# Two decoder layers on one core: down rows in 16 KB pieces, third norm's first half moved beside the last output product, slots computed before gates

## The reference, cut to what matters

```python
x = x + swa(rms_norm(x, od_norm1))        # 16 query heads, 2 key/value heads of 64, window 128
h = rms_norm(x, od_norm2)                 # the third norm that the kernel turns by transposes
logits = h @ w_router                     # 8 experts
top_val, top_idx = lax.top_k(logits, 2)
gates = softmax(top_val) placed at top_idx
for e in range(8):
    y = y + gates[..., e:e+1] * ((silu(h @ w1[e]) * (h @ w3[e])) @ w2[e])   # w1, w3: 1024 x 3584, w2: 3584 x 1024
x = x + y
```

## Time and profile before

| | |
|---|---|
| three runs | 1455.85, 1457.12, 1460.83 us; median 1457.12 |
| profiled execution | 1462.09 us, span 1460.3 us, granted TensorE clock 0.995 |
| busy in the span | PE 1441.4 (99%), PEld 1200.4, DVE 1133.1 (78%), ACT 944.8 (65%), POOL 35.4 |
| DMA | 437.21 MB, 299 GB/s over the span; q1, SP's queue: 180496 packets, 426.11 MB |
| split of half a unit, mean | VectorE 2.272 us (406 of them), ScalarE 1.898 us |
| attention layer / routing / experts | from about 402 / 486 / 508 us on |

### The profile page before, as it was taken

One profiled execution on the slowest core, in us unless ns is written; L12 is line 12 of the kernel. 1 busy time (PEld: TensorE's weight loads), 2 busy tenths in 40 slices (PEclk: granted clock), 3 DMA queues, 4 the chain that ended last, 5 costly groups with the idle time before them and its releaser, 6 DMA issues.

```text
span 1460.3 us, 19714 instructions
## 1 busy us (share of the span) xinstructions
PE 1441.4 (99%) x7542; PEld 1200.4 (82%) x7542; DVE 1133.1 (78%) x968; ACT 944.8 (65%) x844; POOL 35.4 (2%) x22
## 2 busy tenths in 40 slices
PE   9999999999999999999999999999999999999998
PEld 7998888888886787887888888888888888888886
DVE  6985664454476788988888898888888888898895
ACT  7633643443476766766777777777777777677774
POOL 0000000000000000000000001000000000000000
PEclk9999999999999999999999999999999999999999
DMA  9510666544542499999999999999999999999993
GB/s 360 206 58 28 237 220 219 191 172 146 176 162 83 152 362 364 386 364 348 377 368 386 391 373 380 372 375 376 386 383 372 387 393 367 386 389 372 369 391 149
DMA packets 183873, 437.21 MB, mean 299 GB/s; under 512 B 4880, under 2 KB 6416, under 8 KB 183824
## 3 DMA queue, kind: packets, MB, share of 16 engines
q1 hardware_dynamic: 180496, 426.11, 79.1%
q0 software_dynamic: 2336, 8.39, 2.1%
q10 hardware_dynamic: 992, 2.05, 0.4%
HBM read 431.29 MB, written 5.24 MB: 299 GB/s over the span
## 4 chain that ended last, share of the span: by engine, by line
PE 83%; issue 8%; DMA 4%; DVE 4%; ACT 1%; POOL 0%; DVEq 0%; ACTq 0%; SPq 0%; POOLq 0%
PE ps L272 26%; PE ps L274 25%; PE ps L273 25%; DMA raw<-in_od_moe_w 3%; DVE wlo L261 1%; PE ps L452 1%; DMA out<-arena,slot_tok 1%; ACT whi L255 1%; PE ps L991 1%; PE ps L840 0%; PE ps L1188 0%; DVE hTlo L316 0%; PE ps L2102 0%; DVE small L1418 0%; PE ps L333 0%
## 5 line engine op out<-in xcount | busy, mean ns | idle before, releaser
L261 DVE TENSOR_TENSOR wlo<-raw,whi 128x2048 fp32r<-128x2048 f32 x406 | 905.8, 2272 | 170.6 <-ACT whi L255 168.3
L255 ACT CAST whi<-raw 128x2048 fp32r<-128x2048 f32 x406 | 750.5, 1898 | 210.8 <-DMA raw<-in_od_moe_w 151.3
L272 PE MATMUL ps<-whi,hThi 128*128 128x512 f32 (+1 forms) x1240 | 490.2, 395 | 0.3
L274 PE MATMUL ps<-whi,hTlo 128*128 128x512 f32 (+1 forms) x1240 | 482.7, 389 | 0.0
L273 PE MATMUL ps<-wlo,hThi 128*128 128x512 f32 (+1 forms) x1240 | 482.5, 389 | 0.0
L274 PEld LDWEIGHTS ps<-whi,hTlo 128*128 128x128 f32 x1240 | 233.6, 188 | 48.7
L272 PEld LDWEIGHTS ps<-whi,hThi 128*128 128x128 f32 x1240 | 233.8, 189 | 47.3 <-issue 1.2
L273 PEld LDWEIGHTS ps<-wlo,hThi 128*128 128x128 f32 x1240 | 233.9, 189 | 45.8 <-issue 0.2
L272 PE MATMUL ps<-whi,aThi 128*128 128x512 f32 x560 | 219.3, 392 | 0.0
L274 PE MATMUL ps<-whi,aTlo 128*128 128x512 f32 x560 | 218.2, 390 | 0.0
L273 PE MATMUL ps<-wlo,aThi 128*128 128x512 f32 x560 | 217.9, 389 | 0.0
(11 more groups left out here) (308 smaller groups left out, 759.4 us busy)
## 6 DMA issues: line engine op xcount, KB each, us to landing
raw<-in_od_moe_w SPq DMA_DIRECT2D x168, 2048.0 KB, 9.6
raw<-in_ev_ffn_w SPq DMA_DIRECT2D x21, 2048.0 KB, 7.8
raw<-in_ev_w_in SPq DMA_DIRECT2D x6, 2048.0 KB, 13.1
raw<-in_ev_w_out SPq DMA_DIRECT2D x2, 2048.0 KB, 8.5
raw<-in_od_w_in SPq DMA_DIRECT2D x2, 2048.0 KB, 7.8
raw<-in_od_w_out SPq DMA_DIRECT2D x2, 2048.0 KB, 8.1
raw<-in_ev_w_in SPq DMA_DIRECT2D x2, 1024.0 KB, 8.6
xres<-in_x SPq DMA_DIRECT2D x2, 512.0 KB, 4.3
```

The lines of the kernel that those rows point to most:

```text
L255: act.copy(whi[s][:, part], raw[s][:, part]).then_inc(hi_ready, 1)
L261: dve.tensor_tensor(wlo[s][:, part], raw[s][:, part], whi[s][:, part].bitcast(F32), ALU.subtract).then_inc(lo_ready, 1)
L272: pe.matmul(to, lhi, rhi, start=first, stop=False)
L274: return pe.matmul(to, llo, rhi, start=False, stop=last)
```

## The change

It has five parts. (a) `w2m` gives partition p the rows 4p to 4p+3 of a block of 512 instead of rows p, 128+p, 256+p, 384+p, so that a partition's 16 KB lie together in DRAM; the gate product writes its column 4i+c to place c*128+i, so that the transposed blocks fit these rows. (b) ScalarE's and VectorE's parts of the first half of norm 3 stand ahead of the squares and of the last addition, VectorE's split of U_MOE is cut in two around them, and on TensorE the second half is turned behind the router's and `dense`'s first two k instead of ahead of them. (c) The second tile of scaled rows is made behind the copy of the router rows; `dense` of tile 1 gives five k instead of four ahead of the rank products. (d) The gates are computed behind the slots and expert 0's `select` (`gate_values`), with a semaphore `tok_ready` for TensorE's `index`. (e) The second half of norm 2 is turned behind `keys_values`' first two k instead of ahead of them.

```diff
+        def by_row(t):
+            return t.rearrange("p (i c) -> p i c", c=FC)
+        def by_block(t):
+            return t.rearrange("p (c i) -> p i c", c=FC)
-        def dve_scaled(dve, by):
-            for t in range(TT):
+        def dve_scaled(dve, by, tiles):
+            for t in tiles:
...
-        w2m = a["od_moe_w2"][0].rearrange("e (b c p) n -> (e b) p c n", p=P, c=FC)
+        w2m = a["od_moe_w2"][0].rearrange("e (b p c) n -> (e b) p c n", p=P, c=FC)
...
-                    dve.tensor_tensor(actf[0:CAP, t, :], sil[0:CAP, t, :], H3[t][0:CAP, :], ALU.mult).then_inc(a_ready, 1)
+                    dve.tensor_tensor(by_block(actf[0:CAP, t, :]), by_row(sil[0:CAP, t, :]), by_row(H3[t][0:CAP, :]),
+                                      ALU.mult).then_inc(a_ready, 1)
...
             hi_u(act, U_MOE)
+            act_turned(act, 3, 0)
             for t in range(TT):
                 act_square(act, 3, 0, t)
             act_square(act, 3, 1, 0)
-            act.wait_ge(unit_used, U_ROUTER)
-            act_turned(act, 3, 0)
...
                 if n == 3:
-                    lo_u(dve, U_MOE)
+                    split_lo(dve, U_MOE, U_MOE % NS, halves=(0,))
+                    dve_turned(dve, 3, 0)
...
-            dve_turned(dve, 3, 0)
+            split_lo(dve, U_MOE, U_MOE % NS, halves=(1,))
         def odd_tensor(pe):
-            pe_turn_x(pe, 2, 1)
...
                         if b == 3:
                             ins.then_inc((qkv_ps, unit_used)[t], 1)
+                    if b == 0:
+                        pe_turn_x(pe, 2, 1)
...
-            dve_scaled(dve, route_gain)
+            dve_scaled(dve, route_gain, (0,))
...
             dve.tensor_copy(by_expert, ps[4][0:NE, 0:T]).then_inc(rt_rows, 1)
+            dve_scaled(dve, route_gain, (1,))
...
-            dve.wait_ge(rt_exp, 1)
...
             dve.wait_ge(rank_ps, 1)
...
+            def gate_values():
+                dve.wait_ge(rt_exp, 1)
...
+                dve.tensor_tensor(tok_gate[:, :, 0:NE, 1], gate, tmp, ALU.add).then_inc(tok_ready, 1)
...
                 select(q, 0, n0)
                 if q == 0:
+                    gate_values()
                     split_lo(dve, U_MOE + 1, 1)
...
         def experts_tensor(pe):
-            pe_turn_x(pe, 3, 1)
...
-            early, late = range(KD // 2), range(KD // 2, KD)
+            early, late = range(KD // 2 + 1), range(KD // 2 + 1, KD)
...
-            pe.wait_ge(hT_ready, 12 + 2)
             for b in range(4):
                 pe.wait_ge(hT_ready, 12 + b + 1)
...
                 if b < 3:
                     dense(0, (2 * b, 2 * b + 1))
+                if b == 0:
+                    pe_turn_x(pe, 3, 1)
...
                 pe.wait_ge(sel_ready, 2 * n + 2)
+                pe.wait_ge(tok_ready, 1)
```

More of the change, by code:

```diff
@@ L1686, in build_program @@
         rt_rows, rt_ps, first_sil, sil_ps = sem("rt_rows rt_ps first_sil sil_ps")
-        old_in, y_half = sem("old_in y_half")
+        old_in, y_half, tok_ready = sem("old_in y_half tok_ready")
         sil_slots = actf[0:CAP, 1, :]
@@ L1944, in experts_vector @@
             link(dve.tensor_tensor(slot_of[:, :, 0:NE], tmp, ahead, ALU.add))
+            def gate_values():
+                dve.wait_ge(rt_exp, 1)
+                link(dve.tensor_scalar(v[0], second, 1.0, None, ALU.add))
+                link(dve.reciprocal(v[0], v[0]))
+                link(dve.tensor_tensor(v[1], second, v[0], ALU.mult))
+                link(dve.tensor_tensor(gate, oh1, along(v[0], NE), ALU.mult))
+                link(dve.tensor_tensor(tmp, oh2, along(v[1], NE), ALU.mult))
+                dve.tensor_tensor(tok_gate[:, :, 0:NE, 1], gate, tmp, ALU.add).then_inc(tok_ready, 1)
             def select(q, e, n):
@@ L2010, in moe @@
                     dve.wait_ge(sil_ready, tiles(0, 0, 0))
-                    dve.tensor_tensor(actf[0:CAP, 0, :], sil_slots, H3[0][0:CAP, :], ALU.mult).then_inc(a_ready, 1)
+                    dve.tensor_tensor(by_block(actf[0:CAP, 0, :]), by_row(sil_slots), by_row(H3[0][0:CAP, :]),
+                                      ALU.mult).then_inc(a_ready, 1)
                     split_lo(dve, U_MOE + NS, 0)
```

## The result

The forecast was wrong: the changed kernel is slower. Twelve runs of it have a median of 1472.16 us (1466.43 to 1479.39), twelve of the kernel before 1460.62 (1455.85 to 1466.81). The ratio is 1.0092, with a 95% interval of 1.007 to 1.0115. I had forecast 1453.8. The profiled execution took 1479.39 us, the longest of the twelve and 17.3 more than the profiled one of before.

A forecast was written before the change was run, and what follows sets the result against it. The experts' stage runs at TensorE's pace, its three-buffer ring twice late; -1.3 + 0 - 0.6 - 0.6 - 1.7 = -4.2 gives 1457.9 us for the profiled execution. Median forecast 1453.8, between 1452.9 and 1454.8; range 1449.5 to 1460.

The forecast's parts named there:

- Steps 1 to 3: Third norm to first up product: TensorE's idle goes, ranks and gather come earlier; -1.3 us, bounds 0 and -2.2.
- VectorE late next: Ahead of the first up product: TensorE waits 0.7 us for VectorE's split; of 2.2 us only 1.3 to 1.4 arrive.
- Step 4: Second norm, keys and values: 0.34 us idle covered, but later transposes expose a wait; net 0, bounds -0.5 and +0.5.
- Step 6: Experts' gate product, written 512 bytes apart: taken as 0.68 us as now, with 1.4 as the upper bound.
- The cover I named: Experts' settled steps: a 2.5 us margin from gate product to its turn covers the write, except at late turns.
- Step 5: Experts' down loads: 16 KB pieces save 0.24 us of a unit's 5.2, so 0.6 at each of two late turns.
- the 2.9 us that I booked at the late turns: Experts' two late TensorE turns: 0.6 us saved at each, and 1.7 for one clock drop gone.
- The rival "larger pieces are slower": Each expert's down load: at 20% slower, each of some 54 steps pays 0.44 us; about 1477 us, chance 0.10.

The follow-up runs named there:

- halves: Kernel before, with each experts' load from the fourth unit on issued as two 1 MB DMAs with a semaphore each: 1454.09 us, ratio 0.9973.
- halves_no_a: Changed kernel without part (a), with each experts' load from the fourth unit on issued as two 1 MB DMAs: 1451.86 us, ratio 0.9953.
- halves_no_kv: Changed kernel without part (a), experts' loads as two 1 MB DMAs, second norm's transposes back ahead of keys and values: 1453.10 us.
- pieces_only: Kernel before with the down rows in 16 KB pieces alone, the gate product keeping its order: 1472.75 us, ratio 1.0089.

## Why the prediction was wrong, step by step

**Steps 1 to 3 (third norm, scaled rows, slots): right in kind, too small.** I took 1.3 us, with VectorE late next. The trace gives 2.0, and the pair `halves`, `halves_no_a` 2.2 (1454.09 less 1451.86, with step 4). TensorE reached the transposes of the router rows, ranks and the gather at 494.42, 498.24 and 501.55, which is, less the 1.7 of the later start, 492.7, 496.5 and 499.8, where I had said 492.8, 496.9 and 500.2. What I oversized was VectorE's queue: it ended the split of U_MOE + 1 at 506.4, 504.7 on the scale of before, not 505.3, so TensorE waited 0.2 where I had it wait 0.7.

**Step 4 (keys and values): right.** The stall was exchanged for one of 0.29 us idle at 407.32 in the changed kernel; 0.06 by the trace, 0 forecast. The times of `halves_no_kv` missed the half microsecond that I had allowed, for the clock's sake.

**Step 6 (gate product): undersized, and harmless.** I took 0.68 us between 0.68 and 1.4; it is 1.09. The Trainium skill, "Advanced Engine Details and Errata", section "Memory Cachelines", says that an access to another line of 16 bytes each time is penalised, and the trace agrees with 1.09 us against 0.68. The cover I named, the margin ahead of a settled turn, holds: 1.0015 alone, nothing with the halves. With both edits of part (a) it may add a little (1.0116 against 1.0089, and the intervals overlap).

**Step 5 (down rows in 16 KB pieces): this is the step that failed, and in its sign.** "I take the 0.24, because its rows are the same queue and the same tensor." As busy time of the DMA engines that was right: 0.61 us for a piece was what I worked out, 0.611 is the median. But I let 0.24 us of engine time stand for 0.24 us less until a load has landed. What the ring waits for is the last of 16 landings, and these came 0.4 to 0.6 us later, in a kernel with 14 late turns instead of 2. How much of that the pieces bring and how much the late turns themselves is open; that the pieces bring the late turns is shown by `pieces_only` (10 of 55 in its trace). No row of before tells one from the other: the lone unit in the earlier trace rows had the engines to itself, and nothing in flight beside it. So the 2.9 us that I booked at the late turns, the clock included, came with the other sign, as 17.7 in the profiled execution.

**The rival "larger pieces are slower"** had the sign, its place and, at 21 us for 20%, nearly the size; I gave it 0.10. Its mechanism was another, so that its size was luck. It had each step pay an excess once the bytes of a step no longer fit in 16.7 us; the settled steps are still 16.7 and the bytes fit, since with the halves all of the loss is gone. What is paid is late turns, here and there, when a load of 11 to 13 us meets a ring that allows 9.9 (in the chain above all but the load takes 18.73 - 11.90 = 6.8 of the 16.7). I had seen that room in the first part ("so little room in the DMA that a ring of three buffers twice falls behind"), counted what a shorter load would give, and never what one longer by 5% would take: that was the sensitive side, as two late turns in 55 show that the ring lies at the edge.

## What to carry to other kernels

Where a ring of buffers sits at the edge of its time, look at the time from a load's issue to its last landing, among the others in flight, and not only at bytes or packet time; a row of a load alone says nothing on that. Before a descriptor is made larger or its rows are put at a power of two, count how far the ring is from its edge, and cost both signs. If it is at the edge, wait for each load in two halves with a semaphore each: here that was worth 4 us on the kernel before, 20 on the changed one, and with it the size of the pieces no longer matters (the changed kernel without (a), with the halves, takes 1451.86 us, 0.47% under the kernel before).

## What was not expected of the hardware

- Larger packets have less engine time for each byte (80.6 ns for 2 KB at 16 KB packets, 83.4 at 4 KB, 90.1 at 2 KB, in mixed traffic) and still gave the slower kernel; with 2 KB packets for the down rows it was no slower than with 4 KB (0.9982, up to 1.0001).
- With partitions 16 KB apart, 4 KB pieces cost 0.6%; 28 KB apart, nothing measurable (1.0062 and 1.0007; the two also differ in rows read again).
- A VectorE product of 96 x 512 float32 takes 1.09 us instead of 0.68 when neighbours are 512 bytes apart in the result alone, and 1.08 when they are 16 bytes apart in both inputs alone.
- The granted clock can fall in the attention layer as well (0.72 from 443 to 449 us, in `halves_no_kv` and `pieces_only` alone of the eighteen profiles); between `halves_no_a` and `halves_no_kv` it came with 1.2 us.
